# Fill products of the last two layers: fp32 products become three fp32r products of split operands, with GpSimd making the parts of the weights

## The chip, the core and the metric

The kernel is one program on one core of a Trainium2 chip. Its engines run side by side and meet through semaphores: TensorE (PE: matmuls, with the loads of its stationary operand shown apart as PEld), VectorE (DVE), ScalarE (ACT), GpSimd (POOL) and SyncE (SP, which here starts the DMAs of the weights). The metric is the device time of one execution in microseconds, as a median of several runs. All products accumulate in PSUM, which has eight banks here (`ps`); GpSimd works in SBUF alone.

## What is computed

Two transformer blocks over 256 tokens of width 2048, batch 1, in fp32. The first block (a mixer with S5 and RG-LRU branches, then 32 experts) isn't touched by the change. The second has an even and an odd layer, each a projection of the normed tokens, three branches, and one output projection with a residual:

```python
def even_layer(x, mem, rel_table, norm_g, w_in, ...):
    h = rms_norm_2(x, norm_g) @ w_in
    gq, gk, gv, gb, ga, gg, dq, dk, dv, dg, mq, mg = split_cols(h, EV_SPLITS)
    y = jnp.concatenate([
        gdn_branch(gq, gk, gv, gb, ga, gg, conv_w, a_log, dt_bias, gdn_gain),
        diff_attention(dq, dk, dv, dg, rel_table, dq_gain, dk_gain, lam, subln, lambda_init),
        memory_attention(mq, mg, mem, mem_norm, mem_w_kv, mem_qn, mem_kn),
    ], axis=-1)
    return x + y @ w_out

def odd_layer(x, mem, positions, rel_table, norm_g, w_in, ...):
    h = rms_norm_2(x, norm_g) @ w_in
    sq, sk, sv, sg, mlq, ckv, kr, mlg, mq, mg = split_cols(h, OD_SPLITS)
    # window attention, latent attention with rope, memory attention
    return x + y @ w_out
```

## The kernel before

**Stream of weights.** SP streams all big weights in one order (`STREAM`) as units of 1 MB into a ring of eight slots (`k.ring`). A unit holds `UNIT_KC` = 4 chunks of 128 rows by 512 columns. Whoever is the last to need a unit raises `unit_used`, and SP may then load the unit eight places on.

**Dense products** (`gemm_tokens`, and `FeatureSplit` inside `gdn_in`). Each operand is split into a high part (rounded to fp32r) and a low part (the rest, in fp32r). ACT makes the high part of a weight chunk (L353), DVE the low part by a subtraction (L379), and PE multiplies high by high, high by low and low by high (L327 to L329), for each of the two tiles of 128 tokens. So one *step* (one chunk of the inner dimension for a block of 512 columns and all 256 tokens) is 6 matmuls. Four buffers for each part let ACT and DVE run ahead. The activations are split at the start of each such product (L349, L376).

**Fill products** (`Fill`). Between the small and dependent operations of attention, head norms and the delta rule, PE gets steps of other large products, so that it has work while it waits. They are plain fp32 products straight from the ring: 2 matmuls a step (L631, and L3358 for the gate of the GDN branch, written out inside `gdn_heads`), in PSUM banks 6 and 7. A plain fp32 matmul of 128x512 appears in the trace as two records, so a step shows as 4. GpSimd is idle in nearly all of this part. `fill.load`, `fill.multiply`, `fill.store_act` and `fill.store_dve` are called with a number of steps, once for each engine in each section.

**Sections.** The program is a row of sections (`nc.Block`), each with one instruction list for each engine. Between two sections all five engines meet at a barrier, so a section lasts as long as its slowest engine. In the part concerned the order is: `gdn_in` (dense, its last part a tail with convolutions and transposes), `head_norm` for q, `head_norm` for k, `gdn_heads`, `head_norm` of the result, `to_features`; the dense product of the diff branch (6 blocks), a short section that starts the loads of the bias and computes lambda, `head_norm`, `attention`, `head_norm`; memory attention (`head_norm`, `attention`, `times_silu`); the dense output product; the norm of the odd layer; then for the odd layer window attention (dense, `head_norm`, wait for loads, two times `attention`, `times_silu`), MLA (dense, a section with a small product for the rope part of the keys, the up projection, `head_norm`, `mla_rope`, `attention`, `times_silu`), the keys of memory attention (dense), memory attention, and the output product. There are nine head norms, and five stretches of attention (the two of window attention counted as one).

**`head_norm`** runs on DVE: for each part a square (L2458) and a sum over each head (L2460), then a root on ACT, a product with the root's inverse (L2473), sometimes with a gain (L2478) and a gate (L2483). Each of L2458, L2473, L2478 and L2483 is a TENSOR_TENSOR whose two inputs lie in SBUF.

**Keeping PE busy** (`keep_busy`, L266): products of no use that fill PE's idle time, such as the thirty after the small product `ba` (L2369, L2383) in the tail of `gdn_in`.

## Time and profile before

| | us |
|---|---|
| median of 3 runs | 2791.82 |
| lowest, highest | 2789.42, 2791.92 |
| span of the profiled execution | 2787.4 |
| PE busy | 2598.2 (93%) |
| DVE busy | 1354.9 (49%) |
| ACT busy | 976.6 (35%) |
| POOL busy | 105.2 (4%) |

A busy share is an average over all stages. For this change the stretch from 1422 us to the end counts, where the fill products run. A record of a matmul overlaps with its neighbours (the next one starts before it ends), so what a matmul costs is read from the distance between starts, not from its duration.

### The profile page before, as it was taken

Reading aid. Unit: us, or ns where it says so; the run is one execution under the profiler, and the core shown is the slowest. Engines: PE = TensorE matmul, PEld = TensorE weight load, DVE = VectorE, ACT = ScalarE, POOL = GpSimd, SP = SyncE. Lnnn points to the kernel's source line nnn. Section 1 sums busy time; section 2 is a strip of 40 time slices with the busy share of each in tenths; the row PEclk is TensorE's granted clock in tenths of the full one; section 3 lists DMA queues with packets and bytes.
Section 4 is the critical chain, followed back from the end, with each engine's and each line's share of the span. In section 5 each row is a group of like instructions: output and inputs, shape, how many; then the busy total and the mean of one; then the engine's idle time right before and its main releaser. Section 6 shows DMA issues by size and latency. Waiting matters only on the chain. (4 is left out here: it accounts for less than half of the span.)

```text
span 2787.4 us, 38289 instructions
## 1 busy us (share of the span) xinstructions
PE 2598.2 (93%) x14362; PEld 1770.8 (64%) x14362; DVE 1354.9 (49%) x2599; ACT 976.6 (35%) x1730; POOL 105.2 (4%) x117
## 2 busy tenths in 40 slices
PE   8999999999888889999998999989899989988999
PEld 7984555887544444448975766855467746845757
DVE  5654784665311112226764545554535445464535
ACT  5544122444122122225524424432235414423424
POOL 0001111020011100010000000000000000001000
PEclk9999999999999999999999999999999989999999
DMA  7754433554499999984431114543334523431432
GB/s 302 216 211 156 138 138 141 186 199 147 160 422 422 422 421 422 399 344 161 169 122 67 38 57 166 189 173 106 106 136 141 200 85 141 154 122 75 148 109 91
DMA packets 80312, 529.66 MB, mean 190 GB/s; under 512 B 9089, under 2 KB 13569, under 8 KB 18849
## 3 DMA queue, kind: packets, MB, share of 16 engines
q1 hardware_dynamic: 76128, 514.50, 48.9%
q0 software_dynamic: 3456, 11.02, 1.6%
q8 instruction: 99, 1.62, 0.2%
q10 hardware_dynamic: 576, 2.10, 0.2%
q14 instruction: 53, 0.43, 0.1%
HBM read 520.24 MB, written 7.34 MB: 189 GB/s over the span
## 5 line engine op out<-in xcount | busy, mean ns | idle before, releaser
L379 DVE TENSOR_TENSOR split_wl<-ring,split_wh 128x512 fp32r<-128x512 f32 x480 | 331.0, 698 | 227.5 <-ACT split_wh L353 225.7
L353 ACT ACTIVATE split_wh<-ring 128x512 fp32r<-128x512 f32 x480 | 301.0, 631 | 291.6 <-PE ps L329 291.6
L327 PE MATMUL ps<-split_wh,split_xh 128*128 128x512 f32 x960 | 375.5, 391 | 0.0
L329 PE MATMUL ps<-split_wh,split_xl 128*128 128x512 f32 x960 | 373.6, 389 | 0.0
L328 PE MATMUL ps<-split_wl,split_xh 128*128 128x512 f32 x960 | 373.5, 389 | 0.0
L2132 PE MATMUL ps<-ring,yT 128*64 128x256 f32 x2048 | 247.8, 387 | 52.4 <-DMA ring<-in_weights 48.3
L631 PE MATMUL ps<-ring,xT 128*128 128x512 f32 x512 | 241.8, 625 | 29.9 <-issue 7.2
L434 PE MATMUL ps<-features_xh,features_wh 128*128 128x256 f32 x832 | 236.7, 285 | 1.5 <-DVE features_wl L425 1.5
L2132 PEld LDWEIGHTS ps<-ring,yT 128*64 128x64 f32 x2048 | 137.7, 137 | 155.4 <-DMA ring<-in_weights 91.0
L436 PE MATMUL ps<-features_xh,features_wl 128*128 128x256 f32 x832 | 235.3, 283 | 0.0
L631 PE MATMUL ps<-ring,yT 128*128 128x512 f32 x448 | 206.3, 612 | 20.9 <-issue 11.1
L999 PE MATMUL ps<-ring,xT 128*128 128x512 f32 x512 | 222.0, 592 | 2.8 <-PEq L451 1.7
L329 PEld LDWEIGHTS ps<-split_wh,split_xl 128*128 128x128 f32 x960 | 180.2, 188 | 37.5
L327 PEld LDWEIGHTS ps<-split_wh,split_xh 128*128 128x128 f32 x960 | 180.2, 188 | 37.4
L328 PEld LDWEIGHTS ps<-split_wl,split_xh 128*128 128x128 f32 x960 | 180.2, 188 | 37.3
L631 PEld LDWEIGHTS ps<-ring,xT 128*128 128x128 f32 x512 | 99.5, 200 | 150.7 <-issue 142.2
L425 DVE TENSOR_TENSOR features_wl<-ring,features_wh 128x512 fp32r<-128x512 f32 x208 | 139.4, 691 | 83.3 <-ACT features_wh L419 79.5
L419 ACT ACTIVATE features_wh<-ring 128x512 fp32r<-128x512 f32 x208 | 130.2, 630 | 133.5 <-PE ps L436 133.5
L999 PEld LDWEIGHTS ps<-ring,xT 128*128 128x128 f32 x512 | 97.1, 190 | 120.6 <-issue 118.1
L631 PEld LDWEIGHTS ps<-ring,yT 128*128 128x128 f32 x448 | 84.6, 195 | 123.4 <-issue 123.3
L434 PEld LDWEIGHTS ps<-features_xh,features_wh 128*128 128x128 f32 x832 | 159.6, 192 | 2.9 <-DVE features_wl L425 2.6
L436 PEld LDWEIGHTS ps<-features_xh,features_wl 128*128 128x128 f32 x832 | 159.6, 192 | 0.0
(630 smaller groups left out, 3389.9 us busy)
## 6 DMA issues: line engine op xcount, KB each, us to landing
ring<-in_weights SPq DMA_DIRECT2D x468, 1024.0 KB, 5.1
x_res<-in_x SPq DMA_DIRECT2D x1, 2048.0 KB, 7.5
yT<-in_mem SPq DMA_DIRECT2D x1, 2048.0 KB, 15.7
rel_skew<-lru_feat POOLq DMA_DIRECT2D x1, 2048.0 KB, 50.7
mem_features<-yT ACTq DMA_DIRECT2D x4, 512.0 KB, 6.6
s_wb<-in_s_bc POOLq DMA_DIRECT2D x4, 512.0 KB, 4.0
s_wc<-in_s_bc POOLq DMA_DIRECT2D x4, 512.0 KB, 3.9
gate_bias<-in_gate_bias POOLq DMA_DIRECT2D x8, 256.0 KB, 3.9
```

The source lines that it names most:

```text
L327: nc.tensor.matmul(out, xh[:, kc, at], wh[:, c % deep, :], start=kc == 0, stop=False)
L328: nc.tensor.matmul(out, xh[:, kc, at], wl[:, c % deep, :], start=False, stop=False)
L329: last = nc.tensor.matmul(out, xl[:, kc, at], wh[:, c % deep, :], start=False, stop=kc == chunks - 1)
L353: nc.scalar.activation(wh[:, c % deep, :], raw(unit, turn, c), ACT.Copy).then_inc(w_high.sem, 1)
L379: last = nc.vector.tensor_tensor(wl[:, c % deep, :], raw(unit, turn, c), wh[:, c % deep, :], ALU.subtract)
L419: self.k.nc.scalar.activation(self.wh[:, c % self.deep, :], self.k.ring[:, slot, c * BLK:(c + 1) * BLK], ACT.Copy)\
L425: self.k.nc.vector.tensor_tensor(self.wl[:, c % self.deep, :], self.k.ring[:, slot, c * BLK:(c + 1) * BLK], self.wh[:, c % self.deep, :], ...
L434: nc.tensor.matmul(out, self.wh[:, c, cols], self.xh[:, kc, :], start=kc == 0, stop=False)
L436: last = nc.tensor.matmul(out, self.wl[:, c, cols], self.xh[:, kc, :], start=False, stop=kc == KC - 1)
L631: last = nc.tensor.matmul(k.ps[:, 6 + t, :], x[:, kc, t * P:(t + 1) * P], k.ring[:, slot, c * BLK:(c + 1) * BLK], start=kc == 0, stop=kc = ...
L999: mm = nc.tensor.matmul(k.ps[:, 6 + t, :], k.xT[:, kc, t * P:(t + 1) * P], k.ring[:, slot, c * BLK:(c + 1) * BLK], start=kc == 0, stop=kc ...
L2132: last = nc.tensor.matmul(k.ps[s * WIN:(s + 1) * WIN, p, 0:FF], window[:, p, kc, :], k.ring[:, slot, at:at + FF], start=kc == 0, stop=kc = ...
```

## The change

From the first unit behind the experts on (`LATE`), the ring has 4 slots of 1 MB instead of 8. The other half of its memory holds the high and low part of the normed tokens (`k.xh`, `k.xl`), which are made once in each layer and used by every product of that input (`ready=True` leaves the split out). Fill products become `SplitFill`: GpSimd makes the high part of each weight chunk (CAST into `fill_wh`, 8 chunks deep, in the memory of `xT`) and the low part in place of the raw chunk in the ring (`ring_low`); PE multiplies three times. A section whose fill has S steps makes GpSimd prepare S steps, the ones that lie `FILL_LEAD` = 6 ahead of PE; the first six are made beside the dense product in front, and the section that would make the last ones makes fewer. Where the fill's input comes from a branch (three of the fills), `TokenSplit` lets GpSimd split it first: four casts and four subtractions of 128x512.

The number of fill steps stays 256 and so does that of the dense ones, but some change places. The gate of the diff branch (32 steps) leaves the dense product and becomes fill, the output product of the diff branch (32 steps) becomes dense. In the GDN branch 10 of 64 fill steps move into the tail of `gdn_in` (`TAIL_CHUNKS`), where `keep_busy` and the product `ba` stood; `ba` moves into the first block of `gdn_in`. `gdn_heads` goes from 36 fill steps to 26. The section for lambda and the bias loads is dissolved into the dense product. The small product for the rope keys becomes a tiled product inside the dense product of window attention.

```diff
+LATE_RING = 4
+FILL_DEEP = 8
+FILL_LEAD = 6
...
+class SplitFill(Fill):
...
+    def make_high(self, pool, step):
+        k, high, used, n = self.k, self.k.ev("fill_high"), self.k.ev("fill_used"), self.number + step
+        unit_wait(k, pool, self.base + step // UNIT_KC, 0, 0)
+        if n >= FILL_DEEP:
+            pool.wait_ge(used.sem, used.at(n - FILL_DEEP))
+        k.nc.gpsimd.tensor_copy(self.high(step), k.ring[:, self.slot(step), self.columns(step)]).then_inc(high.sem, 1)
+
+    def make_low(self, pool, step):
+        k, high, low, n = self.k, self.k.ev("fill_high"), self.k.ev("fill_low"), self.number + step
+        pool.wait_ge(high.sem, high.at(n))
+        k.nc.gpsimd.tensor_tensor(self.low(step), k.ring[:, self.slot(step), self.columns(step)], self.high(step), ALU.subtract)\
+            .then_inc(low.sem, 1)
+
+    def make(self, pool, steps):
+        self.make_for += steps
+        upto = min(self.make_for + FILL_LEAD, self.first[-1])
+        for step in range(self.made, upto):
+            self.make_high(pool, step)
+            if step > self.made:
+                self.make_low(pool, step - 1)
+        if upto > self.made:
+            self.make_low(pool, upto - 1)
+        self.made = max(self.made, upto)
+
+    def multiply(self, pe, steps):
...
+            pe.wait_ge(low.sem, low.at(self.number + step))
+            for t in range(NT):
+                sums, at = k.ps[:, 6 + t, :], slice(t * P, (t + 1) * P)
+                nc.tensor.matmul(sums, xh[:, kc, at], self.high(step), start=kc == 0, stop=False)
+                mid = nc.tensor.matmul(sums, xh[:, kc, at], self.low(step), start=False, stop=False)
+                last = nc.tensor.matmul(sums, xl[:, kc, at], self.high(step), start=False, stop=kc == chunks - 1)
+            if step % UNIT_KC == UNIT_KC - 1:
+                mid.then_inc(k.unit_used, 1)
+            last.then_inc(used.sem, 1)
...
@@ head_norm
+            @block.gpsimd
+            def _(pool):
+                if fill:
+                    fill.make(pool, steps)
+                if beside is not None:
+                    beside(pool)
...
@@ gdn_in
-                pe.wait_ge(copied.sem, copied.at(final - 1))
-                product.multiply(pe)
-                keep_busy(k, pe, 2, 8)
-                product.add_up(pe)
-                keep_busy(k, pe, 2, 22)
-                pe.wait_ge(evac_a.sem, evac_a.at(final))
-                pe.wait_ge(evac_v.sem, evac_v.at(final))
+                pe.wait_ge(evac_v.sem, evac_v.at(final))
+                fill.multiply(pe, tail[0])
+                pe.wait_ge(copied.sem, copied.at(final - 1))
                 transpose(final, final, range(0, 2))
+                fill.multiply(pe, tail[1])
                 transpose(final, final + 1, range(2, 4))
+                fill.multiply(pe, tail[2])
```

GpSimd's list around the head norms for q and k, in the kernel before. It has nothing in these sections; its rows go from the sections' barriers (L2620 is that of `attention`, L309 that of a dense product) to the next ones:

```order
72 L2076 UNCONDITIONAL_BRANCH
73 L309 UNCONDITIONAL_BRANCH [waits barrier_Pool_Activation_PE_DVE_SP_gather]
74 L2620 UNCONDITIONAL_BRANCH [waits barrier_Pool_Activation_PE_DVE_SP_gather] x2
75 L309 UNCONDITIONAL_BRANCH [waits barrier_Pool_Activation_PE_DVE_SP_gather] x2
76 L2620 UNCONDITIONAL_BRANCH [waits barrier_Pool_Activation_PE_DVE_SP_gather] x2
```

GpSimd's list in the head norm for q, in the kernel after (`fill_wh` is the high part, `ring_low` the low one):

```order
108 L2633 UNCONDITIONAL_BRANCH [waits barrier_Pool_Activation_PE_DVE_SP_gather]
109 L743 CAST fill_wh<-ring 128x512 [waits fill_used,unit_loaded0] x2
110 L748 TENSOR_TENSOR ring_low<-ring,fill_wh 128x512 [waits fill_high]
111 L743 CAST fill_wh<-ring 128x512 [waits fill_used,unit_loaded0]
112 L748 TENSOR_TENSOR ring_low<-ring,fill_wh 128x512 [waits fill_high]
...
118 L748 TENSOR_TENSOR ring_low<-ring,fill_wh 128x512 [waits fill_high] x2
119 L2577 UNCONDITIONAL_BRANCH
120 L2633 UNCONDITIONAL_BRANCH [waits barrier_Pool_Activation_PE_DVE_SP_gather]
```

So GpSimd now has six casts and six subtractions between two barriers, where it had none.

PE's list in the tail of `gdn_in`, before. The dense products (L434 to L436) are followed by the product `ba` (L2369, L2383), products of no use (L266) and the transposes (L3043):

```order
4379 L436 MATMUL ps<-features_xh,features_wl 128x256
4380 L2369 MATMUL ps<-xT,gdn_ba_weights 32x256 [waits loaded,act_b]
4381 L2369 MATMUL ps<-xT,gdn_ba_weights 32x256 x15
4382 L266 MATMUL ps<-rows_sb,ident_sb 128x256 x8
4383 L2383 MATMUL ps<-tiled_stacked,tiled_parts 128x32 [waits parts_copied,stacked]
4384 L2383 MATMUL ps<-tiled_stacked,tiled_parts 128x32
4385 L266 MATMUL ps<-rows_sb,ident_sb 128x256 x22
4386 L3043 MATMUL ps<-ident_sb,gdn_sil 128x128 [waits act_a,evac_v,evac_a]
```

The same place after:

```order
4383 L481 MATMUL ps<-x_high_part,features_wl 128x256
4384 L775 MATMUL ps<-fill_wh,x_high_part 128x512 [waits fill_v,fill_low,fill_a,evac_v]
4385 L776 MATMUL ps<-ring_low,x_high_part 128x512
4386 L777 MATMUL ps<-fill_wh,x_low_part 128x512
4387 L775 MATMUL ps<-fill_wh,x_high_part 128x512
4388 L776 MATMUL ps<-ring_low,x_high_part 128x512
4389 L777 MATMUL ps<-fill_wh,x_low_part 128x512
4390 L775 MATMUL ps<-fill_wh,x_high_part 128x512 [waits fill_low]
```

The product `ba` and the products of no use have left, and PE's first instruction behind the dense products waits for a low part that GpSimd makes.

## Rows read from the trace of the kernel before

**Rows 1.** First part of the page: busy time, share of the span, instructions.
```profile
PE 2598.2 (93%) x14362; PEld 1770.8 (64%) x14362; DVE 1354.9 (49%) x2599; ACT 976.6 (35%) x1730; POOL 105.2 (4%) x117
```
**Rows 2.** PE in time, fill products in the head norm for q: start, duration, instruction.
```profile
1440.04 10.54 PE L631 MATMUL ps<-ring,xT 128*128 128x512 f32 x24 [1.14 <-PEq L3028]
```
**Rows 3.** PE in time, dense product of the diff branch.
```profile
1719.32 0.39 PE L327 MATMUL ps<-split_wh,split_xh 128*128 128x512 f32 x1
...
1720.00 0.39 PE L327 MATMUL ps<-split_wh,split_xh 128*128 128x512 f32 x1
```
**Rows 4.** GpSimd in time, three places where DVE leaves it alone.
```profile
473.18 2.35 POOL L1016 TENSOR_TENSOR gates<-gates,gate_bias 128x1024 f32<-128x1024 f32 x1 [30.14 <-ACT gates L1007]
743.32 2.03 POOL L2302 COPY yT<-moe_room 128x1024 f32 x2 [134.24 <-issue]
1224.17 9.18 POOL L1696 TENSOR_TENSOR yT<-yT,cols_sb 128x256 f32<-128x256 f32 x16 [190.62 <-DMA yT<-mem_features]
```
**Rows 5.** GpSimd in time beside a dense product, and DVE's lines: that stretch, whole run.
```profile
592.71 16.38 POOL L1696 TENSOR_TENSOR mem_for_keys<-mem_for_keys,cols_sb 128x256 f32<-128x256 f32 x16 [117.19 <-DMA mem_for_keys<-mem_features]
L379 DVE TENSOR_TENSOR split_wl<-ring,split_wh 128x512 fp32r<-128x512 f32 x12 | 11.4, 976 | 2.3 <-ACT split_wh L353 2.3
L379 DVE TENSOR_TENSOR split_wl<-ring,split_wh 128x512 fp32r<-128x512 f32 x480 | 331.0, 698 | 227.5 <-ACT split_wh L353 225.7
```
**Rows 6.** DVE and GpSimd in time, 361 to 366 us.
```profile
361.43 1.22 DVE L1613 SCALAR_TENSOR_TENSOR yT<-s_turn,s_part_r 128x1024 f32<-128x1024 f32 x1
361.77 3.08 POOL L1016 TENSOR_TENSOR gates<-gates,gate_bias 128x1024 f32<-128x1024 f32 x1 [16.78 <-ACT gates L1007]
362.56 3.37 DVE L1614 SCALAR_TENSOR_TENSOR yT<-s_turn,s_part_i 128x1024 f32<-128x1024 f32 x1
```
**Rows 7.** Nine head norms by windows (span, busy by engine; sums); sums of DVE's L2458, L2473, L2478, L2483.
```profile
1971.30:1992.80 21.50, 19.54 (x58) 10.24 (x58) 16.54 (x19) 6.58 (x8) 0.00 (x0) 0.92 0.34 111
sum 138.00, PE 127.36 PEld 55.90 DVE 100.01 ACT 17.85 POOL 0.00; mean PE 14.15 PEld 6.21 DVE 11.11 ACT 1.98 POOL 0.00
sum 138.00, DVE 26.62; mean DVE 2.96
sum 138.00, DVE 25.40; mean DVE 2.82
sum 138.00, DVE 8.15; mean DVE 0.91
sum 138.00, DVE 4.72; mean DVE 0.52
```
**Rows 8.** Windows: span, busy PE, PEld, DVE, ACT, POOL, PE clock, DMA; sum is five attentions.
```profile
1422.50:1440.00 17.50, 16.40 (x105) 13.64 (x104) 9.31 (x23) 3.47 (x7) 0.00 (x0) 1.00 0.17 61
1461.70:1667.80 206.10, 190.62 (x2662) 138.75 (x2662) 103.21 (x250) 75.33 (x203) 0.00 (x0) 0.98 0.15 52
1703.40:1835.70 132.30, 132.29 (x584) 109.30 (x583) 73.12 (x105) 64.93 (x104) 0.00 (x0) 1.00 0.54 192
1835.70:1839.10 3.40, 0.00 (x0) 0.00 (x0) 0.91 (x5) 1.55 (x3) 0.00 (x0) 1.00 0.40 117
1856.00:1971.30 115.30, 107.46 (x384) 56.55 (x384) 49.14 (x110) 30.00 (x86) 0.00 (x0) 0.99 0.31 109
2425.50:2433.40 7.90, 7.33 (x64) 7.22 (x64) 1.51 (x5) 2.82 (x6) 0.00 (x0) 1.00 0.01 2
2477.10:2507.60 30.50, 22.86 (x48) 9.63 (x48) 14.69 (x41) 3.71 (x6) 0.00 (x0) 0.89 0.30 104
sum 355.90, PE 315.58 PEld 175.83 DVE 139.75 ACT 97.43 POOL 9.59; mean PE 63.12 PEld 35.17 DVE 27.95 ACT 19.49 POOL 1.92
```
**Rows 9.** PE in time: tail of gdn_in, and a fill step in memory attention after an idle.
```profile
1422.50 1.93 PE L2369 MATMUL ps<-xT,gdn_ba_weights 128*32 128x256 f32 x32
...
1428.29 9.74 PE L266 MATMUL ps<-rows_sb,ident_sb 128*128 128x256 f32 x44
...
2014.19 3.56 PE L631 MATMUL ps<-ring,yT 128*128 128x512 f32 x4 [2.60 <-issue]
```

477 lines of the change are left out of this document (289 added, 188 removed).

## Prediction, written before the changed kernel was run

> **What bounds the kernel now.** I began with the page's busy shares: PE is busy 93% of the span, GpSimd 4% [rows 1]. So the kernel is bound by PE, and by the places where PE waits. The change spends the idle engine to make PE's fill steps cheaper, and the two prices decide. I read them from the engines in order of time. In the head norm for q, 24 records (6 steps) of fp32 fill take 10.54 us, where the last record's end runs over by some 0.3 us: 10.24 / 6 = 1.707 us a step [rows 2]. In a dense product three fp32r matmuls take 1720.00 - 1719.32 = 0.68 us, so 6 matmuls, one step, take 1.364 us [rows 3]. A fill step thus gets 0.343 us cheaper on PE; 256 of them make 88 us, the most that the price alone can bring.
>
> Then GpSimd. Alone, a TENSOR_TENSOR of 128x256 takes 9.18 / 16 = 0.57 us and one of 128x1024 takes 2.35 us, so one of 128x512 takes 1.17 us; two copies of 128x1024 take 2.03 us, a half one then some 0.6 us, with a fixed part allowed for [rows 4]. A step costs GpSimd p = 1.77 us, and that is **more than PE's old 1.707 us**. GpSimd must make S steps in each section with S steps of fill, because all engines meet at its end; the lead of six is only handed on. Where the fill runs back to back, GpSimd sets the time.
>
> Third, GpSimd and DVE disturb each other. Sixteen multiplications on GpSimd take 16.38 us beside a dense product, not 9.18, and DVE's subtraction takes 976 ns there, 698 on average [rows 4, 5]. At 361.77 us GpSimd starts beside a DVE operation that still has 0.88 us to go, and takes 3.08 us, not 2.35; DVE's next one takes 3.37 us, not 1.22, and ends 1.08 us after GpSimd [rows 4, 6]. So a DVE operation with two SBUF inputs and a GpSimd operation run after one another. Call c the part of DVE's time that GpSimd loses: the second place gives 0.73 / 0.88 = 0.83; the first gives 7.2 us lost over 12 operations of 0.70 and two of about 1.2 us, 7.2 / 10.8 = 0.67. I take c = 0.8, since the head norms' operations are long like those of the second place.
>
> **The change part by part.** Bounds are for c = 0 and for c = 1 with longer waits.
>
> *Head norms.* Nine of them last 138.0 us, and DVE's four kinds of operation with two SBUF inputs take 26.6 + 25.4 + 8.2 + 4.7 = 64.9 us of it [rows 7]. After, GpSimd has 66 steps there (6, 6, 10, 8, 2 + 6, 6, 8, 8, 6) and once the split of an input, four more pairs: 70 x 1.77 = 124 us. With 0.8 x 64.9 = 52 us lost to DVE, and 7 us before their work starts (some 0.4 us each, and a longer wait in window attention, an estimate from the 1.14 us at [rows 2]), they take 183 us: **+45 us**. If nothing is lost, GpSimd needs 131 us and the sum is -4; with c = 1 it is 196 us, +58. The worst is the last one of the diff branch, 21.5 us before [rows 7]: 12 pairs of operations, 21.2 us, and 10 us lost to DVE.
>
> *Attention.* The five stretches last 355.9 us, of which PE is busy 315.6 [rows 8]. Of their 116 fill steps, 0.343 each is 40 us, if PE sets all of it. In the diff branch it doesn't: 48 steps need 85 us on GpSimd, and if half of DVE's 49.1 us has two SBUF inputs (an estimate), c adds 20, with gaps 108 us instead of 115.3: -7. The two memory attentions have 20 steps each, 35.4 us on GpSimd plus some 4 for DVE, against PE's 43 us less 7: I take -5 each. Window attention and MLA wait for chains of DVE more than for PE (63 us of 145 are other work and gaps, an estimate): -4 and -1. Sum **-22** (-40 to -6).
>
> *Tail of `gdn_in`.* It lasts 17.5 us, in which PE does the product `ba` (1.93 us) and 9.74 us of work of no use [rows 8, 9]. Ten fill steps, 13.6 us, find room there. But GpSimd can be 8 steps ahead at most, since it has 8 buffers, and must have made 16 by the end: 8 x 1.77 = 14.2 us from the moment PE uses the first, some 3 us in, beside DVE's 9.3 us of convolution with two inputs each. `ba` costs its 2.5 us earlier. **+9** (+2 to +10).
>
> *`gdn_heads`.* 206.1 us, PE busy 190.6 [rows 8]. Ten of 36 steps leave and 26 get cheaper: 10 x 1.707 + 26 x 0.343 = 26 us of PE. Five of the ten stand at the start, where DVE's and ACT's chain for the decay sets the time (I count 3 us of their 8.5), and about three in gaps that PE then waits through. GpSimd has 26 steps in over 180 us and isn't in the way. **-15** (-22 to -11).
>
> *`mla_rope`.* 30.5 us, PE busy 22.9; DVE's chain sets the time [rows 8]. GpSimd makes 12 steps, 21 us, beside 35 short operations of DVE, each of which may have to wait for the one in work. **+6** (-1 to +12).
>
> *Sections without GpSimd's work.* The last section of each fill has 24 steps in all, each cheaper: **-8**. *Wait for the bias:* **+2** (0 to +3).
>
> *Dense products.* The number of steps is the same. GpSimd's first six steps of each fill stand beside one, twice with an input's split: DVE 0.70 us and half a pair, 0.89 us, alternate, 1.59 us for a step in place of 1.364, for some 19 us each, half of it hidden by four buffers. The tiled rope product costs twice `ba`'s 1.93 us, as half as many run side by side. **+6** (+3 to +11). DMA moves 192 GB/s at 54% busy there [rows 8], and a unit lasts PE 5.5 us, so I cost the ring of four at nothing; its cover is that half of the DMA's time.
>
> *Removed sections.* Lambda's section goes, 3.4 us; the rope product's section shrinks from 7.9 to about 5 us, the length of its root [rows 8]. **-6**.
>
> Sum: 45 - 22 + 9 - 15 + 6 - 8 + 2 + 6 - 6 = **+17 us** against the span of 2787.4. The median of the runs lies 4.4 us above the span, so 2804.4 + 4.4 = 2809 us. With all lower bounds the sum is -4 - 40 + 2 - 22 - 1 - 8 + 0 + 3 - 6 = -76, with all upper ones 58 - 6 + 10 - 11 + 12 - 8 + 3 + 11 - 6 = +63.
>
> The trace's two places give c = 0.67 and 0.83. The Trainium skill, page "SBUF — State Buffer", section "Who interferes with whom", says more: the port pair is an exclusive lock for the whole instruction, so c would be 1. By that rule the sum would lie at its upper bounds, +63 us, by the rows at +17; I take the rows, because both places show some overlap.
>
> **The rivals.** *GpSimd keeps up* (faster). The port costs less, because DVE's operations fall in GpSimd's gaps. Deciding is c: between c = 0, -76 us, and c = 0.8, +17 us, the sum passes zero near c = 0.65, which the first place nearly gives. At c = 0.3 it is some -40 us: 2752. For it speaks that GpSimd has six steps ready at each section's start; against it, that this lead never shrinks and so saves nothing.
>
> *The cast is dear.* No row shows a cast into fp32r on GpSimd. If it costs as much as an operation with two inputs, 1.17 us instead of 0.6, a step costs 2.34 us, and about 160 steps that GpSimd sets (the head norms, the diff and the memory attentions, the tail) cost 0.57 us more: +90, so 2900. Below nothing it can't cost less than the copy.
>
> *PE's clock falls.* PE now waits a little in each step. After an idle of 2.60 us, a fill step's four records took 3.56 us where 1.71 is usual, a clock of 1.2 instead of 2.4 GHz [rows 9]. Ten such stretches would add some 20 us: 2829. Against it, the new gaps are about 0.4 us each.
>
> **How the numbers follow.** The forecast (c from 0.65 to 1, cast like a copy) 0.52, time 2809, own range 2792 to 2850; GpSimd keeps up 0.25; the dear cast 0.12; clock and other costs 0.11. A difference of 0.2% (5.6 us) is about what can be told from none. Of the forecast's 0.52 some 0.05 lies below 2786 and 0.09 within 0.2%; of the rival that keeps up 0.22 is faster, and 0.03 same. So faster 0.27, same 0.12, slower 0.61. The range from 2740 to 2870 leaves out the cheapest end of the one rival and the dear cast.
>
> **What would show it.** Right: GpSimd busy some 500 us; its subtraction at 1.17 us or more, its cast at 0.6; the head norm for q at 15 us, not 10.9; DVE's 1.23 us operations at 1.8 or more there; PE waiting in the head norms for GpSimd; `gdn_heads` under 195 us. Wrong: head norms under 12 us with S = 6 (then c is small), a cast over 1 us, or PE waiting for the ring's DMA in dense products, which I cost at nothing.

## The result and the profile after

The changed kernel takes **2880.2 us** (median of 4 runs, 2873.6 to 2883.6) beside 2790.8 us for the kernel before: a ratio of 1.032, 95% interval 1.031 to 1.034. It is slower, as forecast, but by 89 us and not by 18, and it lies above the range. One of the four executions of `doubles` (below) was in a slow state, 3734 us at a granted clock of 0.645, and isn't counted in its median. The profiled execution has a span of 2876.3 us, beside 2787.4. First line of its page, as [rows 1]:

```profile
PE 2549.1 (89%) x14786; PEld 1886.4 (66%) x14786; DVE 1468.1 (51%) x2585; ACT 968.8 (34%) x1719; POOL 676.7 (24%) x645
```

PE is busy 49 us less and still ends 89 us later. GpSimd has gained 571 us. DVE has 14 instructions fewer than before and is busy 113 us more: it waits while it counts as busy. The costliest groups of GpSimd, and of DVE one whose work is unchanged (698 ns on average at [rows 5]); columns are line, engine, operation, count, then busy time and mean, then idle:

```profile
L748 POOL TENSOR_TENSOR ring_low<-ring,fill_wh 128x512 fp32r<-128x512 f32 x256 | 356.1, 1395 | 0.0
L743 POOL CAST fill_wh<-ring 128x512 fp32r<-128x512 f32 x256 | 210.4, 827 | 940.5 <-DMA ring<-in_weights 628.9 <-PE ps L777 274.5 <-POOLq L3496 9.4
L413 DVE TENSOR_TENSOR split_wl<-ring,split_wh 128x512 fp32r<-128x512 f32 x480 | 347.0, 731 | 240.4 <-ACT split_wh L383 238.5
```

The nine head norms by windows (span, then busy time of PE, PEld, DVE, ACT, POOL, PE's granted clock, DMA; here the first, the worst, and the sum), as [rows 7]:

```profile
1456.00:1471.20 15.20, 8.42 (x36) 6.68 (x36) 11.81 (x10) 2.09 (x3) 14.82 (x12) 0.92 0.42 138
1958.80:1989.00 30.20, 17.93 (x74) 14.82 (x74) 20.65 (x17) 6.66 (x9) 29.12 (x25) 0.83 0.28 104
sum 186.20, PE 103.15 PEld 82.16 DVE 134.41 ACT 18.52 POOL 178.12; mean PE 11.46 PEld 9.13 DVE 14.93 ACT 2.06 POOL 19.79
```

GpSimd is busy 178 of 186 us: it sets the end of nearly every one, as the prediction had it (183 us). GpSimd needs 1.80 us for a step where DVE leaves it alone (below), 126 us for the 70 casts and 70 subtractions here, so by this estimate 52 us are lost, 0.80 of the 64.9 us that DVE's two-input operations take at [rows 7]: the c of the prediction. The attention of the diff branch, and the sum of the five attentions, as [rows 8]:

```profile
1838.60:1958.80 120.20, 101.11 (x480) 80.09 (x480) 63.38 (x107) 28.94 (x84) 90.91 (x96) 0.89 0.28 97
sum 380.30, PE 308.85 PEld 242.70 DVE 178.65 ACT 96.49 POOL 216.11; mean PE 61.77 PEld 48.54 DVE 35.73 ACT 19.30 POOL 43.22
```

The sum of 355.9 us at [rows 8] can't be set beside this one. It is short by some 9 us at the ends of the two memory attentions: each lasts 52.4 us, up to its barrier, with 47.7 us of PE, where the prediction had 43. Taken from barrier to barrier, before and after:

```profile
sum 366.10, PE 323.99 PEld 179.60 DVE 144.54 ACT 97.46 POOL 9.59; mean PE 64.80 PEld 35.92 DVE 28.91 ACT 19.49 POOL 1.92
sum 381.00, PE 308.85 PEld 242.71 DVE 178.66 ACT 96.51 POOL 216.11; mean PE 61.77 PEld 48.54 DVE 35.73 ACT 19.30 POOL 43.22
```

Here the forecast failed: the attentions grew by 15 us, and were to shrink by 22. GpSimd isn't full (90.9 of 120.2 us in the diff branch), PE is busy 15 us less than before, but DVE is busy 178.7 us where it was 144.5.

### The profile page after: what moved, and what is told of

Read it like the earlier page. It is cut to its first block and busy times, and to the rows that moved or that the text cites. A ratio compares the mean times of both kernels' runs of the same rounds, so it can differ in the third digit from the quotient of the medians.

```text
span 2876.3 us, 39414 instructions
## 1 busy us (share of the span) xinstructions
PE 2549.1 (89%) x14786; PEld 1886.4 (66%) x14786; DVE 1468.1 (51%) x2585; ACT 968.8 (34%) x1719; POOL 676.7 (24%) x645
## 5 line engine op out<-in xcount | busy, mean ns | idle before, releaser
L743 POOL CAST fill_wh<-ring 128x512 fp32r<-128x512 f32 x256 | 210.4, 827 | 940.5 <-DMA ring<-in_weights 628.9
L748 POOL TENSOR_TENSOR ring_low<-ring,fill_wh 128x512 fp32r<-128x512 f32 x256 | 356.1, 1395 | 0.0
L353 PE MATMUL ps<-split_wh,x_high_part 128*128 128x512 f32 x672 | 267.5, 398 | 2.9 <-DVE split_wl L413 2.9
L354 PE MATMUL ps<-split_wl,x_high_part 128*128 128x512 f32 x672 | 266.0, 396 | 0.0
L355 PE MATMUL ps<-split_wh,x_low_part 128*128 128x512 f32 x672 | 266.0, 396 | 0.0
L2285 PEld LDWEIGHTS ps<-ring,yT 128*64 128x64 f32 x2048 | 137.8, 137 | 155.5 <-DMA ring<-in_weights 91.1
L775 PE MATMUL ps<-fill_wh,x_high_part 128*128 128x512 f32 x384 | 171.7, 447 | 64.7 <-PEq L2577 31.2
L1152 PE MATMUL ps<-ring,xT 128*128 128x512 f32 x512 | 222.0, 592 | 2.8 <-PEq L496 1.7
L776 PE MATMUL ps<-ring_low,x_high_part 128*128 128x512 f32 x384 | 161.8, 421 | 0.0
L777 PE MATMUL ps<-fill_wh,x_low_part 128*128 128x512 f32 x384 | 160.3, 417 | 0.0
L353 PEld LDWEIGHTS ps<-split_wh,x_high_part 128*128 128x128 f32 x672 | 127.0, 189 | 34.6 <-issue 4.1
```

Source lines behind the costliest of these rows:

```text
L353: nc.tensor.matmul(out, xh[:, kc, at], wh[:, c % deep, :], start=kc == 0, stop=False)
L354: nc.tensor.matmul(out, xh[:, kc, at], wl[:, c % deep, :], start=False, stop=False)
L355: last = nc.tensor.matmul(out, xl[:, kc, at], wh[:, c % deep, :], start=False, stop=kc == chunks - 1)
L743: k.nc.gpsimd.tensor_copy(self.high(step), k.ring[:, self.slot(step), self.columns(step)]).then_inc(high.sem, 1)
L748: k.nc.gpsimd.tensor_tensor(self.low(step), k.ring[:, self.slot(step), self.columns(step)], self.high(step), ALU.subtract)\
L775: nc.tensor.matmul(sums, xh[:, kc, at], self.high(step), start=kc == 0, stop=False)
```

## How GpSimd and DVE meet

DVE and GpSimd in time, head norm for q:

```profile
1458.26 1.28 POOL L748 TENSOR_TENSOR ring_low<-ring,fill_wh 128x512 fp32r<-128x512 f32 x1
1458.64 1.99 DVE L2584 TENSOR_TENSOR yT<-gdn_cv 128x1024 f32<-128x1024 f32 x1
1459.49 1.60 POOL L743 CAST fill_wh<-ring 128x512 fp32r<-128x512 f32 x1
1460.70 1.22 DVE L2586 TENSOR_REDUCE head_stat<-yT 128x8 f32<-128x1024 f32 x1
1461.06 1.29 POOL L748 TENSOR_TENSOR ring_low<-ring,fill_wh 128x512 fp32r<-128x512 f32 x1
```

DVE's multiplication takes 1.23 us alone. It comes 0.90 us before the end of GpSimd's subtraction and takes 1.99. The next cast takes 0.60 us alone, comes 1.14 us before DVE's end, and takes 1.60: 1.00 of 1.14 us is lost. The reduction, with one input, takes 1.22 us beside a subtraction of 1.29: neither loses anything. So two such operations run one after the other almost wholly: DVE loses 0.76 of 0.90 us (0.84) and GpSimd 1.00 of 1.14 us (0.88, the c of this place). Here they take turns. In the memory attention they don't:

```profile
2050.32 1.27 POOL L748 TENSOR_TENSOR ring_low<-ring,fill_wh 128x512 fp32r<-128x512 f32 x1
2050.83 4.29 DVE L639 TENSOR_TENSOR x_res<-yT,x_res 128x512 f32<-128x512 f32 x1
2051.53 0.61 POOL L743 CAST fill_wh<-ring 128x512 fp32r<-128x512 f32 x1
2052.10 2.48 POOL L748 TENSOR_TENSOR ring_low<-ring,fill_wh 128x512 fp32r<-128x512 f32 x2
2055.23 0.47 PE L775 MATMUL ps<-fill_wh,tokens_xh 128*128 128x512 f32 x1 [3.96 <-issue]
```

DVE's addition, 0.68 us of work, starts at 2050.83 and ends at 2055.12, only after GpSimd has run out of buffers at 2054.58. It is the last of the two operations that store the fill's sums, so PE waits 3.96 us for it. In `halves` (below) the same addition takes 6.53 us. The same place with GpSimd writing memsets of like length (`portfree`, below):

```profile
1993.55 0.69 DVE L638 TENSOR_TENSOR x_res<-ps,x_res 128x512 f32<-128x512 f32 x1 [7.79 <-ACT yT L635]
1994.15 0.68 DVE L639 TENSOR_TENSOR x_res<-yT,x_res 128x512 f32<-128x512 f32 x1
1994.47 0.53 POOL L745 MEMSET own_w<- 128x512 f32 x1
1994.93 0.47 PE L780 MATMUL ps<-x_high_part 128*128 128x512 f32 x1 [0.34 <-issue]
```

The Trainium skill, page "SBUF — State Buffer", section "Who interferes with whom", states that a DVE instruction with two SBUF inputs contends with a GpSimd instruction that reads SBUF, not with one that only writes, and that `tensor_reduce` never contends on trn2. These rows agree in all three points.

GpSimd's own price is read from the distance between starts, as its records overlap like PE's. Shortly before that place, where DVE leaves it alone:

```profile
2040.73 0.61 POOL L743 CAST fill_wh<-ring 128x512 fp32r<-128x512 f32 x1
2041.30 1.29 POOL L748 TENSOR_TENSOR ring_low<-ring,fill_wh 128x512 fp32r<-128x512 f32 x1
2042.54 0.61 POOL L743 CAST fill_wh<-ring 128x512 fp32r<-128x512 f32 x1
```

A step takes 2042.54 - 2040.73 = 1.81 us, mostly 1.80: 0.57 for the cast and 1.23 for the subtraction.

## Experiments

All times are medians; ratios are against the kernel before, run on the same chip.

| kernel | what differs | us | ratio, 95% interval |
|---|---|---|---|
| plain | after, fills in fp32, GpSimd makes nothing | 2790.1 | 1.000 [0.999, 1.001] |
| nopool | after, GpSimd makes nothing | 2733.2 | 0.979 [0.978, 0.981] |
| portfree | after, GpSimd writes memsets instead | 2776.3 | 0.995 [0.994, 0.997] |
| no_cast | after without the casts | 2825.1 | 1.013 [1.011, 1.014] |
| after | | 2880.2 | 1.032 [1.031, 1.034] |
| beside | plain, and GpSimd's operations beside it | 2952.5 | 1.059 [1.057, 1.060] |
| memsets | plain, and memsets beside it | 2844.7 | 1.020 [1.018, 1.022] |
| halves | pieces of 128x256 | 2910.6 | 1.044 [1.042, 1.045] |
| doubles | pieces of 128x1024 | 2909.9 | 1.042 [1.040, 1.044] |
| warm | PE's waits filled, too much | 2936.9 | 1.054 [1.052, 1.055] |
| warm_b | the right count | 2886.3 | 1.036 [1.034, 1.037] |
| warm_c | and in the right place | 2879.0 | 1.032 [1.030, 1.033] |
| plain_rope | plain, rope product in its old place | 2785.8 | 0.9993 [0.9985, 1.0002] |
| own_parts | and x's parts in memory of their own | 2781.5 | 0.9971 [0.9960, 0.9982] |
| swapped | plain_rope, ring and x's parts change halves | 2787.1 | 0.9994 [0.9984, 1.0003] |

**The whole in four steps.** The first four kernels split the change.

`plain`:

```diff
-                nc.tensor.matmul(sums, xh[:, kc, at], self.high(step), start=kc == 0, stop=False)
-                mid = nc.tensor.matmul(sums, xh[:, kc, at], self.low(step), start=False, stop=False)
-                last = nc.tensor.matmul(sums, xl[:, kc, at], self.high(step), start=False, stop=kc == chunks - 1)
+                last = nc.tensor.matmul(k.ps[:, 6 + t, :], x[:, kc, t * P:(t + 1) * P], k.ring[:, self.slot(step), self.columns(step)],
+                                        start=kc == 0, stop=kc == chunks - 1)
...
     def make(self, pool, steps):
-        self.make_for += steps
...
+        pass
```

> The changed kernel with its fill products as before, in fp32 from xT and yT: PE does not use the parts, GpSimd makes none, and no part of an input is made. What stays of the change is all that it moves: the ring of four slots, the shared parts of x in the dense products, the fill steps in the tail of gdn_in, the moved gate and rope products, the removed sections. Nothing of the computation is left out. My theory (GpSimd's operations are what costs, by the barrier at the section's end, by DVE's time and by PE's clock) expects a kernel faster than the one before: 6 us from removed sections, some 10 to 15 us from PE work that now stands in the tail instead of work of no use and out of gdn_heads, 2 us back for the rope product: 2765 to 2780 us, PE's clock at 0.98 or above, attentions at 350 to 360 us in sum. The rival (the ring of four slots or the moved work costs the time) expects 2810 us or more, with PE waiting for DMA or a low clock still there.

It measured 2790.1 us. All that the change moves brings nothing: both readings missed. Where it went is shown at the end of this section.

`nopool`:

```diff
-            pe.wait_ge(low.sem, low.at(self.number + step))
+            unit_wait(k, pe, self.base + step // UNIT_KC, 0, 0)
...
-                mid = nc.tensor.matmul(sums, xh[:, kc, at], self.low(step), start=False, stop=False)
+                mid = nc.tensor.matmul(sums, xh[:, kc, at], any_l, start=False, stop=False)
...
     def make(self, pool, steps):
-        self.make_for += steps
...
+        pass
```

> The changed kernel with PE's six fp32r matmuls a step as they are, but without GpSimd's casts and subtractions: PE multiplies columns of x's parts in their place (the computation of the fill products is left out, its shape and its wait for the ring's DMA stay). It prices PE's side alone. Between this and the one with plain fp32 fill products lie at most 88 us (256 steps at 0.343 us). I expect 50 to 80 us of them, since DVE's chains set the time in parts of the attentions: 2700 to 2725 us. The rival (six short matmuls with six weight loads a step don't run at the pitch of a dense product between other matmuls, so PE's side is worth little) expects less than 25 us below the plain one, 2750 us or more.

2733.2 us, 57 us below the plain one, as expected, though the time itself lies 8 us above its range, since the plain one did: the split form is worth two thirds of 88 us on PE, if its operands come for nothing.

`beside`, and `memsets` with two memsets for each subtraction and one for each cast:

```diff
+    k.nc.gpsimd.tensor_copy(k.own[:, n % 4, :], k.rows[:, 0:BLK])
+    k.nc.gpsimd.tensor_tensor(k.own[:, 4 + n % 4, :], k.rows[:, 0:BLK], k.own[:, n % 4, :], ALU.subtract)
```

> Fill products in fp32 on PE, and GpSimd's 256 casts and 256 subtractions of 128x512 in the same sections, in the same order and as far ahead, but on inputs and outputs that nobody waits for (PE's fill products read other data of the same shape, so their results are left out). It costs GpSimd's work alone: DVE's lost time, the barrier at each section's end, and what PE's idles do to its clock. PE's step is 1.71 us here instead of 1.36, and no wait ties PE to GpSimd within a section. My theory expects the changed kernel's time nearly whole, 2860 to 2900 us, with head norms at 180 to 190 us in sum and attentions at 370 us or more. The rival (the coupling costs the time: PE waits for single buffers, step by step) expects 2790 to 2820 us, since GpSimd's 2.2 us a pair is then hidden in most sections but the head norms.

> As the one with GpSimd's work beside plain fill products, but each cast is a memset of 128x512 and each subtraction two of them: GpSimd is as busy in the same places and reads no SBUF, it only writes; no input's parts are made. Results of the fill products are left out. No row of the trace shows such a memset's time; if it takes 0.4 to 0.6 us, a step costs GpSimd 1.2 to 1.8 us. Theory one (DVE loses its time to any GpSimd operation) expects DVE's multiplications in the head norms at 1.8 us or more and the time within 30 us of the kernel with casts and subtractions. Theory two (only GpSimd operations that read, or that have two inputs, take DVE's time) expects DVE's operations there at 1.25 us, the attentions at 350 to 360 us in sum, and 2770 to 2800 us.

2952.5 us, above both readings, and 2844.7 us: with memsets DVE's multiplications in the head norms take 1.23 us, as theory two had it, but the time lies 45 us above its range. With memsets DVE is busy 1354.5 us (1344.4 without any), with casts and subtractions 1444.2: nearly all that DVE loses, it loses to operations that read. The 10 us that memsets take lie in operations with one input. A TENSOR_SCALAR of the diff attention, in `plain` and in `memsets`:

```profile
L2896 DVE TENSOR_SCALAR att_scores<-att_scores,att_stat 128x256 f32<-128x256 f32 x16 | 4.9, 348 | 0.0
L2911 DVE TENSOR_SCALAR att_scores<-att_scores,att_stat 128x256 f32<-128x256 f32 x16 | 8.6, 580 | 0.0
```

Both totals overstate the cost in the changed kernel: GpSimd was released there by whole units of four steps, and so, as far as this can be told, began later in each section. The gap of 108 us also holds the longer work (1.80 instead of 1.41 us a step between starts, and the split of the inputs). `portfree` therefore keeps the changed kernel's own waits.

`portfree`:

```diff
-        k.nc.gpsimd.tensor_copy(self.high(step), k.ring[:, self.slot(step), self.columns(step)]).then_inc(high.sem, 1)
+        k.nc.gpsimd.memset(k.own_w[:, n % 2 * 4, :], 0.0).then_inc(high.sem, 1)
...
-        k.nc.gpsimd.tensor_tensor(self.low(step), k.ring[:, self.slot(step), self.columns(step)], self.high(step), ALU.subtract)\
+        for m, width in enumerate((BLK, BLK, 416)):
+            last = k.nc.gpsimd.memset(k.own_w[:, n % 2 * 4 + 1 + m, 0:width], 0.0)
```

> The changed kernel in its structure, with the same waits between GpSimd and PE, but GpSimd's cast is one memset of 128x512 (0.53 us) and its subtraction three memsets, 512, 512 and 416 columns, some 1.3 us by the memset's row: 1.85 us a step, as long as cast and subtraction take where DVE leaves them alone. Nothing of the ring is read by it, so the results of the fill products are left out; PE multiplies columns of x's parts. The profile with memsets beside fp32 products showed DVE's times unchanged, so what this saves against the changed kernel (2880 us) is what the two engines take from each other, and what it costs against the one without GpSimd's work (2733 us) is GpSimd's bare time at the section's ends and buffers. My theory (the bare time was in the prediction's sum, the mutual exclusion was mis-sized) expects 2790 to 2815 us, so 65 to 90 us for the exclusion. The rival (bare time, waits and barriers are most of it) expects 2835 us or more.

2776.3 us, below both readings. GpSimd is as busy in the diff attention as in the changed kernel, and DVE is not:

```profile
1807.20:1910.60 103.40, 94.88 (x480) 75.75 (x480) 52.92 (x107) 29.00 (x84) 90.62 (x192) 0.95 0.32 113
sum 345.30, PE 296.76 PEld 234.73 DVE 149.25 ACT 96.48 POOL 215.38; mean PE 59.35 PEld 46.95 DVE 29.85 ACT 19.30 POOL 43.08
sum 148.60, PE 107.44 PEld 85.59 DVE 99.98 ACT 18.45 POOL 129.52; mean PE 11.94 PEld 9.51 DVE 11.11 ACT 2.05 POOL 14.39
```

The first row is the diff attention (120.2 us in the changed kernel, with GpSimd busy 90.9), the second the five attentions (380.3), the third the nine head norms (186.2). Without GpSimd's work the five attentions take:

```profile
sum 336.20, PE 296.28 PEld 231.95 DVE 140.71 ACT 96.32 POOL 9.55; mean PE 59.26 PEld 46.39 DVE 28.14 ACT 19.26 POOL 1.91
```

The spans of the profiled executions thus give, from before to after: moves +1.7 (2787.4 to 2789.1), PE's cheaper products -56.6 (2732.5), GpSimd's bare time +45.0 (2777.5), what GpSimd and DVE take from each other **+98.8** (2876.3). The 98.8 are rather too few: a step of memsets takes 2.00 us between starts where the two operations take 1.80 (1458.44 to 1460.44 us in `portfree`), and memsets still cost DVE 12 us of busy time (1343.6 to 1356.0), in operations such as the TENSOR_SCALAR above. They also hold what PE's clock loses by the longer waits. By sections, worked out from PE's restarts behind the barriers in the timelines:

| us | before | plain | nopool | portfree | after |
|---|---|---|---|---|---|
| up to the norm for q | 1440.0 | 1444.0 | 1439.6 | 1442.8 | 1456.0 |
| norms for q and k | 22.2 | 25.0 | 19.0 | 25.1 | 30.4 |
| gdn_heads | 205.8 | 197.3 | 190.4 | 192.9 | 195.5 |
| GDN norm, features | 33.4 | 31.7 | 26.1 | 35.5 | 39.5 |
| diff norms, attention | 153.9 | 149.8 | 140.7 | 146.2 | 173.6 |
| two memory norms, attentions | 126.7 | 125.0 | 113.9 | 124.8 | 137.6 |
| window norm, attention | 98.8 | 98.9 | 89.2 | 94.3 | 108.4 |
| MLA norm, rope, attention | 114.4 | 113.8 | 114.0 | 113.7 | 131.2 |
| last section of each fill | 49.8 | 49.6 | 45.7 | 47.9 | 46.0 |
| dense products and norms | 542.3 | 554.2 | 553.9 | 554.2 | 558.1 |

**Which of GpSimd's operations.** `no_cast` leaves out the cast, so that GpSimd only subtracts:

```diff
-        k.nc.gpsimd.tensor_copy(self.high(step), k.ring[:, self.slot(step), self.columns(step)]).then_inc(high.sem, 1)
```

> The changed kernel without GpSimd's casts: it only subtracts, 256 times 128x512, from the ring, other data of the same shape, and for inputs too; PE multiplies columns of x's high part where the cast's output stood (that part of the fill products' computation is left out). It shows what is left if another engine made the high parts for nothing. GpSimd's bare work falls from 1.87 to 1.27 us a step, under PE's 1.36, and it takes half as many turns with DVE. If turns and lengths both count, as the pieces of other sizes suggest, more than half of the 147 us that GpSimd's work cost goes: 2780 to 2810 us, and a head norm with 6 steps takes 12 to 13 us. The rival (the subtraction, with its two inputs, does nearly all of the harm) expects 2835 us or more.

2825.1 us: the cast costs 55 of the 147 us that GpSimd's work costs, the subtraction 92, roughly as their lengths (0.57 and 1.23). Neither reading holds as it stood: an engine that made the high parts for nothing would still leave the kernel slower than before.

**Pieces of another size.** `halves`:

```diff
-        k.nc.gpsimd.tensor_copy(self.high(step), k.ring[:, self.slot(step), self.columns(step)]).then_inc(high.sem, 1)
+        for at in (slice(0, SEQ), slice(SEQ, BLK)):
+            last = k.nc.gpsimd.tensor_copy(self.high(step)[:, at], ring[:, at])
+        last.then_inc(high.sem, 1)
```

> The changed kernel with each of GpSimd's casts and subtractions as two of 128x256. GpSimd's work stays the same in sum (an operation with two inputs of 128x256 takes 0.57 us, half of 1.17), but each operation that a short one of DVE's must wait for is half as long. Theory one (DVE's chains of many short operations are stretched by one whole GpSimd operation each) expects attentions and the rope section shorter by 10 to 25 us in sum and head norms unchanged: 2855 to 2870 us. Theory two (the two engines' sum of times is what counts, whatever the pieces) expects 2875 us or more, since nothing is saved and each piece has a fixed part.

`doubles`:

```diff
-        for step in range(self.made, upto):
+        for step in range(self.made, upto, 2):
...
+        both, at = slice(n % FILL_DEEP, n % FILL_DEEP + 2), slice(step % UNIT_KC * BLK, (step % UNIT_KC + 2) * BLK)
+        k.nc.gpsimd.tensor_copy(k.fill_wh[:, both, :].rearrange("p a b -> p (a b)"), k.ring[:, self.slot(step), at]).then_inc(high.sem, 2)
```

> The changed kernel with one cast and one subtraction of 128x1024 for two steps in place of two of each of 128x512. With pieces of 128x256 the time rose by 30 us, and the head norms by 1.4 to 2.6 us each: by the rows the two engines take turns, operation by operation, so each of GpSimd's operations waits for one of DVE's where these come back to back. If turns are what is counted, half as many of them give most of it back with the other sign: head norms 1 to 3 us shorter each, 2850 to 2868 us. Against it stands that a short DVE operation waits for up to 2.4 us, and PE gets its buffers in pairs, later: the rival expects the attentions longer by more than that, 2880 us or more.

2910.6 and 2909.9 us, 30 us slower both, as the rival reading had it each time. The minimum, median and maximum of each operation in ns, cast and subtraction, for 128x256, 128x512 and 128x1024:

```profile
L745 POOL CAST fill_wh<-ring x512: 386/398/2509, 1408.9 to 2812.0; 128x256 fp32r<-128x256 f32 x171
L753 POOL TENSOR_TENSOR ring_low<-ring,fill_wh x512: 712/730/2321, 1411.0 to 2814.4; 128x256 fp32r<-128x256 f32 x171
...
L743 POOL CAST fill_wh<-ring x256: 600/612/2722, 1409.6 to 2785.2; 128x512 fp32r<-128x512 f32 x128
L748 POOL TENSOR_TENSOR ring_low<-ring,fill_wh x256: 1253/1286/2766, 1411.0 to 2787.5; 128x512 fp32r<-128x512 f32 x128
...
L744 POOL CAST fill_wh<-ring x128: 1029/1041/3126, 1411.0 to 2818.4; 128x1024 fp32r<-128x1024 f32 x128
L750 POOL TENSOR_TENSOR ring_low<-ring,fill_wh x128: 2337/2388/4192, 1412.1 to 2820.0; 128x1024 fp32r<-128x1024 f32 x128
```

By the distance between undisturbed starts a step costs GpSimd 2.08, 1.80 and 1.76 us (2061.03 to 2063.11 us in `halves`, 2061.72 to 2065.24 for two steps in `doubles`). My expectation that halves cost the same in sum was wrong: two more instructions a step cost 0.28 us, an estimated 0.14 us of fixed part each. Small pieces make GpSimd's work longer (busy 751 us, 677, 615) and spare DVE (1446 us, 1468, 1533); large ones the reverse. They don't end the long waits: in `halves` the addition above takes 6.53 and 5.92 us in the two memory attentions. In `doubles` each cast is also followed at once by its own subtraction, which has to wait 0.15 us for it. The piece of 128x512 is the better of the three, and no size makes the sum fit.

**PE's clock.** The granted clock fell from 0.985 to 0.961; counted as time at the lower level, 2 x 0.015 x 2787 = 84 us and 2 x 0.039 x 2876 = 224 us. Behind a wait of 6.94 us the fill for k starts at the lower level: 0.63 us for a matmul that takes 0.39 at the full clock.

```profile
1471.96 0.63 PE L776 MATMUL ps<-ring_low,x_high_part 128*128 128x512 f32 x1
```

`warm`, `warm_b` and `warm_c` fill such waits with useless matmuls:

```diff
                 elif fill:
                     fill.multiply(pe, steps)
+                    keep_busy(k, pe, 5, warm)
```

> The changed kernel with useless matmuls of 128x256 (0.22 us each at the full clock) behind the fill products of the nine head norms, and behind those of mla_rope, where PE otherwise waits for GpSimd: 24, 15, 50, 36, 38, 20, 26, 50, 45 and 20 of them. They fill PE's waits of 4 to 13 us and leave the waits inside the attentions. It tells what PE's clock costs there: the profile shows the fill at half clock behind such waits. If the clock is a cause of its own, the time falls by 10 to 30 us, to 2850 to 2870 us, with head norms as long as they are and the sections behind them shorter. The rival (the sections at half clock are bound by GpSimd or DVE all the same) expects 2874 us or more, the head norms unchanged.

> As the one with useless matmuls in PE's waits, with the right count: one of these fp32 matmuls took 0.43 us, not 0.22 (100 records, 21.74 us for 50), so there the useless work was longer than the waits, and 57 us slower than the changed kernel. Now 13, 9, 20, 16, 18, 9, 14, 25, 20 and 9 of them, 4 to 11 us each, at most as long as the waits. If the clock is a cause of its own, 2850 to 2870 us, with the products behind those waits at the full clock. The rival (the sections are bound by GpSimd and DVE) expects 2874 to 2886 us, though the granted clock rises.

> As the one with useless matmuls of the right count (2886 us), but in mla_rope the 26 of them stand ahead of the last four fill steps, where PE waits 13.0 us for DVE's store, and not behind them, where they made the section 9.3 us longer. If PE's clock behind these waits is a cause of its own beyond that, 2860 to 2872 us. The rival, which that run supports (its other sections with filled waits were 0 to 4 us shorter, others 2 us longer), expects 2872 to 2882 us, no more than 8 us from the changed kernel's 2880.

`warm` was mis-sized by a factor of two. I had read 44 records as 44 matmuls, but an fp32 matmul leaves two records. The 50 in the MLA norm are 100 records and take 21.74 us, 0.43 us each:

```profile
2562.83 21.74 PE L290 MATMUL ps<-rows_sb,ident_sb 128*128 128x256 f32 x100
```

`warm_b` had the right count and still took 2886.3 us: in the rope section the useless matmuls stood behind the fill, and the section took 43.9 us instead of 35.5. With the right count and place (`warm_c`) the same fill for k runs at the full clock:

```profile
1472.22 0.39 PE L776 MATMUL ps<-ring_low,x_high_part 128*128 128x512 f32 x1
```

and the kernel takes 2879.0 us, where the changed one takes 2880.2. The norm for k still ends when GpSimd ends. So the clock behind the head norms' waits costs nothing in sum that these runs could tell, though the sections behind them moved both ways (memory attention of the even layer 56.3 to 51.4 us, diff attention 120.5 to 123.3, `gdn_heads` 195.3 to 198.1). What it costs inside the attentions (0.89 there, 0.95 in `portfree`) isn't separated from DVE's delays, which make the waits.

**Where the moved work's gain went.** `plain_rope` undoes one of the moves:

```diff
-            gemm_tokens(k, k.xT, 5, KC // UNIT_KC, *store_tokens(k, ps), parts=parts, product=product,
-                        ahead=lambda sp: load(k, sp, kr_w, k.dram["mla_kr_w"]), beside=beside)
+        gemm_tokens(k, k.xT, 5, KC // UNIT_KC, *store_tokens(k, ps), parts=parts)
...
-            rms_scale(k, ckv, ckv, n=KV_RANK, squares=squares)
+            rms_scale(k, ckv, ckv, n=KV_RANK, squares=squares, fill=product)
```

> The kernel with fp32 fill products and all that the change moves (2790 us), with the rope product back in the section of its root, as before. Nothing is left out. Moving it cost 6.8 us in the window branch's dense product (116.3 to 123.1 us) and 2.1 us ahead of the product upwards, and gave back 1.5 us in the section it left. So 7 us less than the one with fp32 fill products: 2782 to 2785 us, 0.2 to 0.3% faster than the kernel before. The rival (those 7 us come from the ring of four slots) expects 2788 to 2792 us and the same dense product at 122 us or more.

2785.8 us, 4 us below plain and not to be told from the kernel before. The window branch's dense product fell from 123.1 to 118.7 us, but stayed 2.4 us above before. The rest is a slower dense product. PE in time at the same kind of place, first in `plain`, then in `own_parts`:

```profile
2130.07 0.40 PE L354 MATMUL ps<-split_wl,x_high_part 128*128 128x512 f32 x1
2130.31 0.39 PE L355 MATMUL ps<-split_wh,x_low_part 128*128 128x512 f32 x1
2130.54 0.39 PE L353 MATMUL ps<-split_wh,x_high_part 128*128 128x512 f32 x1
2130.77 0.39 PE L354 MATMUL ps<-split_wl,x_high_part 128*128 128x512 f32 x1
```

```profile
2129.82 0.39 PE L354 MATMUL ps<-split_wl,split_xh 128*128 128x512 f32 x1
2130.05 0.39 PE L355 MATMUL ps<-split_wh,split_xl 128*128 128x512 f32 x1
2130.27 0.39 PE L353 MATMUL ps<-split_wh,split_xh 128*128 128x512 f32 x1
2130.50 0.39 PE L354 MATMUL ps<-split_wl,split_xh 128*128 128x512 f32 x1
```

Three matmuls take 0.70 us with x's parts in the ring's former half and 0.68 us with parts in memory of their own, as at [rows 3]. 336 steps of 6 matmuls make 13 us. In these products x's parts are the stationary operand. In `gdn_in`, where they are the moving one, three matmuls take 0.360 us in `before` and in `plain` alike.

`own_parts`:

```diff
-        gemm_tokens(k, k.xT, 5, KC // UNIT_KC, *store_tokens(k, ps), parts=parts)
+        gemm_tokens(k, k.xT, 5, KC // UNIT_KC, *store_tokens(k, ps))
```

> The kernel with fp32 fill products and the rope product in its old place (2786 us), in which five of the six dense products after the GDN branch (out of the even stage, window, MLA, memory keys and the last) have parts of x in memory of their own again, as before, and make them anew; gdn_in and the diff branch's product keep theirs in the ring's former half. Nothing is left out. In the traces three matmuls of a dense product take 0.700 us where their x parts lie in the ring's former half, and 0.680 us before and in the product upwards, which has its own. 272 steps of 6 matmuls at 0.04 us less make 11 us. If the place of the parts is the cause, 2774 to 2778 us and a pitch of 0.680 in these five: 0.4 to 0.5% faster than the kernel before. The rival (the ring of four slots, whose DMA lands closer behind PE, slows the matmuls) expects 0.700 still, and 2785 to 2789 us.

`swapped`:

```diff
-        parts_at = ring_at + 4 * LATE_RING * UNIT_KC * BLK
+        parts_at = ring_at
...
-    return at % (RING if at < LATE else LATE_RING)
+    return at % RING if at < LATE else at % LATE_RING + 4
```

> As the kernel with fp32 fill products and the rope product in its old place, but the ring's four late slots lie in its upper half and x's parts in its lower half. Nothing is left out. It parts two readings of the 0.700 us: if it is the address of the parts, they now lie where the ring was read from before, and the pitch changes to 0.680 us (some 2773 us); if it is that parts and ring share a region, whichever way round, or that the parts lie right beside what DMA writes, the pitch stays 0.700 us and the time 2784 to 2789 us. I take the second as likelier, 0.6 to 0.4.

In `own_parts` the pitch is 0.680 us in the five products with parts of their own and 0.70 in the diff branch's, which keeps the ring's half: the place of the parts is the cause, the ring's four slots aren't. The kernel takes 2781.5 us, 4 us below `plain_rope` where I expected 8 to 12. The five products are 9.7 us shorter in sum, their parts made anew included (between barriers 71.6 to 70.0, 115.6 to 112.8, 93.2 to 91.1, 48.7 to 47.5 and 74.9 to 72.9 us). But 3.3 us are lost ahead of the first of them, where the edit changes nothing (the diff branch's product starts at 1699.7 us, not 1696.4), and 1.3 us in the norm of the odd layer; neither is explained. It is **faster than both kernels**, by 0.29% against the one before (interval 0.18 to 0.40%), without any of the split fill products. `swapped` keeps 0.70 us and 2787.1 us: either half of the ring is slow. What about that memory slows PE by 3% stays open; no other place was tried.

## Why the prediction was wrong

The span was forecast to grow by 17 us and grew by 89. Of the 72 us between, attention makes 37, the dense products and removed sections 16, the stretch up to the norm for q 7, `gdn_heads` 5, the sections without GpSimd's work 4; the rest is small.

- **Attention**: -22 forecast, +15 measured (366.1 to 381.0 us). This is the step that failed, and it failed twice. It started from 40 us of gain on PE and took off 18, for GpSimd's pace with c in it and for DVE's own chains. The runs give a gain of 29 with no work on GpSimd (337.4 us between the same barriers) and of 20 with bare work (346.5), and then the exclusion costs 35. I let c cost GpSimd time and asked only whether GpSimd then sets the pace. I never charged what DVE loses. DVE's chain (staging q and k, norm of the scores, storing the fill's sums) is what PE waits for there: in the diff branch PE is idle for 19 us of 120.2, for 8.5 of 103.4 in `portfree`. Without its first wait, which begins in the head norm ahead, PE waits 10.4 us in all for DVE's staging there, and 2.0 us in `portfree`. Of the 35 us, 23 are PE's idle time and 12 are records of the same matmuls that last longer, as they do at a lower clock. That -20 without exclusion lies near -22 confirms nothing: the -22 already held 20 us of c in the diff branch.
- **GpSimd's price**: 1.77 us a step forecast, 1.80 measured between starts. Right. The cast costs 0.57 and the subtraction 1.23 us, forecast at 0.6 and 1.17; the records, 0.61 and 1.29 by their medians, are longer because they overlap. The rival of the dear cast is out.
- **Head norms**: +45 forecast, 138.0 to 186.2 us, +48 measured. Right, mechanism and size: the 52 us lost to DVE came as forecast, by c = 0.80. With memsets the norms take 148.6 us, +11, but a step of memsets is 0.2 us longer, 14 us over 70 of them, so the split of the 48 us into 11 and 38 gives the exclusion too little.
- **Tail of `gdn_in`**: +9 forecast. PE's last dense product ends 6.8 us later than before, and from there to the norm for q it takes 26.7 us instead of 17.5: the +9 came true. The 6.8 us, where the prediction had 2.5 for `ba`, aren't `ba`'s: `portfree` has moved it too and is 0.1 us behind. GpSimd's first casts and subtractions run there beside the last dense block, whose splits and convolution on DVE they hold up. In the tail, too, it is the same mechanism: DVE's eight operations of the convolution take 3.75 us in `portfree` and twice that here.

```profile
1424.26 3.75 DVE L3286 SCALAR_TENSOR_TENSOR gdn_raw<-gdn_cv,cols_sb,gdn_raw 128x256 f32<-128x256 f32 x8
```

```profile
1430.95 7.68 DVE L3280 SCALAR_TENSOR_TENSOR gdn_raw<-gdn_cv,cols_sb,gdn_raw 128x256 f32<-128x256 f32 x8
```

- **`gdn_heads`**: -15 forecast, -10 measured, -8.5 of it from the ten steps that left. Cheaper products gave 7 us more without GpSimd's work (190.4 us) and kept 2 of them with it.
- **Rope**: +6 forecast, 30.5 to 35.5 us, +5. Right: PE waits 13.0 us for DVE's chain to store the first block's sums, 7.2 before.
- **Wait for the bias** in window attention: +2 forecast, 4.8 to 8.2 us, +3.
- **Sections without GpSimd's work**: -8 forecast, -4 measured.
- **Dense products and removed sections**: +6 and -6 forecast, +16 measured together. 13 is the matmuls' pitch with x's parts in the ring's half, a term put at nothing, which no row of the trace before could show. The tiled rope product cost 3.7 us of PE and gave back 1.6 in the two sections behind (10.6 to 9.0 us). The product of the memory keys, beside which GpSimd splits the fill's input, took 54.0 us instead of 48.6 in `plain`. Lambda's section gave back its 3 us. PE didn't wait for the ring's DMA in dense products, as forecast.
- **The rival that GpSimd keeps up** had the wrong foot: even with next to nothing lost between the two engines (`portfree`) the span is 10 us below before and not 76. With no row for PE's gain where GpSimd only just keeps up, I had priced it nearly in full. The exclusion as a whole I had at 93 us (from -76 to +17), and it measured 99. So in the whole it was the base of the sum that missed, by 66 us: some 20 in the attentions, 15 each in the dense products and in the head norms (there at most, by the longer memsets), 9 in `gdn_heads`.
- **PE's clock**: the time at the lower level grew by 140 us, not by the 40 that ten stretches at 20 us of loss would have, yet by `warm_c` those behind the head norms cost nothing in sum.

## What to carry to other kernels

Before an idle GpSimd gets work, list DVE's operations with two SBUF inputs in the same stretch, and follow who waits for DVE: beside such operations, work that reads SBUF on GpSimd costs nearly as much as if DVE did it, and one short operation on DVE can wait through several of GpSimd's. Compare the helper's price per step with what the step costs today (1.80 against 1.71 us here) before counting what the helped engine saves. A memset of the same length on the helper, in the same place with the same waits, splits the cost of time from the cost of the port in one run, up to the one-input operations that memsets delay too. And end the windows of before and after at the same barriers: 9 us here were a window that ended too soon.

## What the runs showed of the hardware

- A DVE operation is not always let in after one of GpSimd's: 0.68 us of work took 4.29 us, until GpSimd paused, and 6.53 us in `halves`.
- GpSimd's memsets took nothing from DVE's operations with two SBUF inputs: with 390 us of them (`memsets`) DVE's convolution stayed at 479 ns, while casts and subtractions (`beside`) made it 557. They did delay a TENSOR_SCALAR with one such input: 348 ns alone, 580 in `memsets`, 629 in `portfree`.
- fp32r matmuls of 512 columns took 0.70 us for three in place of 0.68 where x's parts, their stationary operand, lie in either half of the ring's memory. Where the parts are the moving operand, in `gdn_in`, the place made no difference (0.360 us for three).
